# A hybrid decoder step on one core: roots ahead of conversions, the first gate slab in halves, a unit-wise tail, and sampled attention with stationary probabilities

## The chip, the cores and the metric

The kernel runs on one core of a Trainium2 chip. The metric is device time in microseconds, as the median of several executions. The profile is of one execution.

## The reference

One layer of a decoder for 256 prompt tokens and 8 sampled sequences of 4 tokens, 288 tokens in all. The input is normed and multiplied by `w_in` (2048 x 5632); eight heads go through a gated linear recurrence (HGRN2, state 128 x 128), sixteen query heads over four key heads through attention with a window of 128, a learned bias and a sink; both go through `w_out` and a SwiGLU.

```python
u = rms_norm(x, norm_g) @ w_in
qa, fa, ia, ga, qb, kb, vb = jnp.split(u, SPLIT_POINTS, axis=-1)
oa, st_p = hgrn2_scan(qa, lf, ka, va, state)       # prompt: zeros; sampled: state_hgrn
ob = swa(q, k, v, sink, bias, mask)                # sampled: over 128 cached keys + 4 new
x = x + jnp.concatenate([hgrn2_output(oa), ob], axis=-1) @ w_out
h = rms_norm(x, g)
y = x + (jax.nn.silu(h @ wg) * (h @ wu)) @ wd      # d_ff 5632
```

## The kernel before

All activations lie transposed: 128 features on the partitions, 288 tokens (`T`) on the free axis. Every weight is read once, in 192 slabs of 128 x 2048 numbers (1 MB). A slab takes three steps: SyncE loads it into one of three `raw` buffers; ScalarE rounds it to `wh` (`high`, L628), the high half; VectorE subtracts and gets the low half `wl` (`low`, L973). Activations have halves as well (`act_h`, `act_l`). TensorE's `passes` then does for each of 16 blocks of a slab high x high (L1514) and high x low (L1515), and after a wait for the low half (`between`) low x high (L1518): 48 matmuls of 288 columns into one PSUM bank. The load of slab s waits for the split of slab s - 3, the conversions wait through `unit_done` for TensorE's use of the buffer.

Slabs 0 to 43 are `w_in` (keys and queries of attention, f from 12, q from 20, i from 28, g from 36), 44 to 59 `w_out`, and then the FFN: gate and up slabs in turn, and down slabs of four output tiles each, chunk by chunk (`ffn_walk`). Each engine walks the same loop over s in an order written out by hand. TensorE does the small work at the start of a slab (`at_start`) and ahead of its low pass (`in_the_middle`).

Small work that the change touches, in order:

- Start: `x_squares` (ScalarE) sums squares of three token tiles, `root(1)` takes the root, VectorE inverts it, and `spread_rms` on TensorE in the middle of slab 2 spreads it over partitions. Only then can unit 0 be scaled on its way out of PSUM (`evacuate`), squared on ScalarE, and after it ScalarE did `high(3)`.
- Slab 10: `qk_rows` (mean of the q/k squares), `root(2)`, reciprocal; `qk_broadcast` (L1555) on TensorE in slabs 11 and 12, used by `qk_norm` on VectorE. `high(12)` stood at the end of step 9, `root(2)` in step 10.
- Slab 28 (`S_SA + 4`): sampled attention. `sampled_probs` transposes the probabilities, ScalarE copies them, `sampled_out` multiplies cached and new values (stationary, 64 columns) by them (16 columns moving), for each of four key heads one matmul of new tokens (L1656) and eight of cached ones (L1659). `s_out_copy` writes the head-major result `s_out`; `s_out_low` its low half. GpSimd then zeroes the level buffers, and after `s_out_low` loads the recurrence's states.
- Slabs 29 to 36 (`S_LV`): the recurrence's levels 0 to 7. `level` (L1690, sampled part L1701) computes products, `level_merge` (L1186) puts them under a mask, `level_up` (L1207, L1220 to L1222) scales q, k and f for the next. PSUM banks `mx` are shared, so TensorE waits for merges.
- `w_out`, then the first gate slab: `x2_high` and `x2_low` make the halves of the sixteen tiles of x. Tiles 8 to 15 go to the places that `w_out`'s last matmuls read, so they start after these. `passes_as_they_come` does all high blocks (L1528), `x2_ssq` (L1833), the low weights (L1531), the low activations (L1534).
- The end: `y_group` transposes four tiles of the result at a time (L1993), ScalarE and VectorE copy, SyncE stores; group 3 stands behind the last pass.

## Time and profile before

| | us |
|---|---|
| median of 3 runs (1365.98 to 1367.83) | 1367.4 |
| the profiled execution | 1367.65 |
| its span | 1365.9 |
| TensorE busy | 1352.0 |
| VectorE busy | 768.2 |
| ScalarE busy | 533.0 |
| GpSimd busy | 117.0 |

Times in rows are microseconds from the span's start. PE is TensorE's matmuls, PEld its weight loads, DVE VectorE, ACT ScalarE, POOL GpSimd, SP SyncE. A matmul in full single precision (`f32` operands that are not rounded) leaves two records. Records of matmuls overlap: the distance from start to start is the pace, the duration holds the latency too.

### The profile page before, as it was taken

How to read it: one execution, taken by the hardware profiler on the slowest of the kernel's cores; microseconds unless marked ns; L12 is line 12 of the kernel's file. 1: busy time of each engine (PE TensorE's matmuls, PEld its weight loads, DVE VectorE, ACT ScalarE, POOL GpSimd, SP SyncE). 2: the span in 40 equal slices, each digit the busy share in tenths (PEclk: the TensorE clock that was granted, in tenths of full speed). 3: DMA queues.
4: the chain of work that ended last, by engine and by line, in shares of the span. 5: the costliest groups of instructions: out<-in, count | busy, mean ns of one | idle time of the engine just before them, and what ended most of it. 6: DMA issues, size and time to landing. Idle time of an engine off the chain costs nothing.

```text
span 1365.9 us, 25119 instructions
## 1 busy us (share of the span) xinstructions
PE 1352.0 (99%) x11030; PEld 1317.2 (96%) x11030; DVE 768.2 (56%) x976; ACT 533.0 (39%) x615; POOL 117.0 (9%) x153
## 2 busy tenths in 40 slices
PE   9999999999999999999999999999999999999998
PEld 7999999898899999999999999999999999999998
DVE  5346765588737566446464555546464555545464
ACT  6337975323244344333333333333333333333331
POOL 2010430213200350000000000000000000000000
PEclk8999999899999999999999999999999999999999
DMA  9795545546853555555565565555565565555552
GB/s 286 198 311 156 162 130 151 154 112 180 245 201 124 185 155 155 163 177 155 161 179 155 173 166 156 164 175 155 163 177 155 168 171 156 164 174 155 164 176 71
DMA packets 320744, 231.42 MB, mean 169 GB/s; under 512 B 5126, under 2 KB 292111, under 8 KB 320314
## 3 DMA queue, kind: packets, MB, share of 16 engines
q1 hardware_dynamic: 314432, 206.19, 52.6%
q0 software_dynamic: 6112, 23.59, 5.3%
q8 instruction: 87, 1.43, 0.4%
q14 instruction: 23, 0.19, 0.0%
q10 hardware_dynamic: 90, 0.02, 0.0%
HBM read 219.99 MB, written 14.97 MB: 172 GB/s over the span
## 4 chain that ended last, share of the span: by engine, by line
PE 95%; DMA 2%; DVE 2%; issue 1%; ACT 1%; SPq 0%; ACTq 0%; DVEq 0%
PE acc L1514 29%; PE acc L1518 29%; PE acc L1515 28%; DMA raw<-in_w_in_dram 1%; PE mx L1464 1%; PE mx L1690 1%; PE acc L1528 1%; DMA reg_qkf<-in_x_sample_dram 1%; PE mx L1613 0%; PE mx L1585 0%; PE mx L1659 0%; DVE wl L973 0%; PE mx L1993 0%; PE mx L1773 0%; PE mx L1600 0%
## 5 line engine op out<-in xcount | busy, mean ns | idle before, releaser
L1514 PE MATMUL acc<-act_h,wh 128*128 128x288 f32 x2208 | 596.9, 299 | 1.1 <-ACT wh L628 1.1
L1515 PE MATMUL acc<-act_l,wh 128*128 128x288 f32 x2208 | 593.7, 295 | 0.0
L628 ACT ACTIVATE wh<-raw 128x2048 fp32r<-128x2048 f32 x192 | 366.8, 1911 | 248.3 <-PE acc L1518 234.5
L973 DVE TENSOR_TENSOR wl<-raw,wh 128x2048 fp32r<-128x2048 f32 x192 | 440.2, 2293 | 11.5 <-ACT wh L628 8.1
L1514 PEld LDWEIGHTS acc<-act_h,wh 128*128 128x128 f32 x2208 | 415.5, 188 | 7.2 <-issue 5.0
L1515 PEld LDWEIGHTS acc<-act_l,wh 128*128 128x128 f32 x2208 | 415.0, 188 | 0.0
L1518 PE MATMUL acc<-act_h,wl 128*128 128x288 f32 x2208 | 322.1, 298 | 0.0
L1518 PEld LDWEIGHTS acc<-act_h,wl 128*128 128x128 f32 x2208 | 302.1, 189 | 4.7 <-issue 3.3
L1514 PE MATMUL acc<-mix_h,wh 128*128 128x288 f32 x832 | 228.3, 299 | 0.0
L1515 PE MATMUL acc<-mix_l,wh 128*128 128x288 f32 x832 | 227.7, 295 | 0.0
L1514 PEld LDWEIGHTS acc<-mix_h,wh 128*128 128x128 f32 x832 | 157.1, 189 | 1.7 <-issue 1.7
L1515 PEld LDWEIGHTS acc<-mix_l,wh 128*128 128x128 f32 x832 | 156.4, 188 | 0.0
L1518 PE MATMUL acc<-mix_h,wl 128*128 128x288 f32 x832 | 142.1, 296 | 0.0
L1443 DVE TENSOR_TENSOR reg_x<-acc,reg_x 128x288 f32<-128x288 f32 x176 | 78.9, 455 | 96.9 <-PE acc L1518 96.9
L1518 PEld LDWEIGHTS acc<-mix_h,wl 128*128 128x128 f32 x832 | 120.3, 188 | 0.0
L929 ACT ACTIVATE reg_t<-reg_t 128x288 f32<-128x288 f32 x44 | 19.6, 446 | 186.2 <-DVE reg_t L1408 186.2
L1408 DVE TENSOR_TENSOR reg_t<-acc,reg_t 128x288 f32<-128x288 f32 x44 | 20.2, 459 | 127.3 <-PE acc L1518 127.2
L932 ACT ACTIVATE mix_h<-reg_t 128x288 fp32r<-128x288 f32 x44 | 19.6, 446 | 180.2 <-DVE reg_t L1416 180.2
L1416 DVE TENSOR_TENSOR reg_t<-acc,reg_t 128x288 f32<-128x288 f32 x44 | 20.2, 459 | 119.8 <-PE acc L1518 119.8
L1310 DVE TENSOR_TENSOR reg_x<-acc,reg_x 128x288 f32<-128x288 f32 x32 | 14.3, 453 | 37.5 <-PE acc L1518 37.5
L1420 DVE TENSOR_TENSOR mix_l<-reg_t,mix_h 128x288 fp32r<-128x288 f32 x44 | 20.2, 459 | 22.6 <-ACT mix_h L932 22.6
L1410 DVE TENSOR_TENSOR reg_t<-reg_t 128x288 f32<-128x288 f32 x44 | 20.2, 459 | 22.6 <-ACT reg_t L929 22.6
(265 smaller groups left out, 714.6 us busy)
## 6 DMA issues: line engine op xcount, KB each, us to landing
raw<-in_w_in_dram SPq DMA_DIRECT2D x44, 1024.0 KB, 5.9
raw<-in_w_gate_dram SPq DMA_DIRECT2D x44, 1024.0 KB, 5.6
raw<-in_w_up_dram SPq DMA_DIRECT2D x44, 1024.0 KB, 5.7
raw<-in_w_down_dram SPq DMA_DIRECT2D x44, 1024.0 KB, 5.1
raw<-in_w_out_dram SPq DMA_DIRECT2D x16, 1024.0 KB, 5.4
reg_x<-in_state_hgrn_dram POOLq DMA_DIRECT2D x16, 256.0 KB, 6.3
out_dram<-reg_x POOLq DMA_DIRECT2D x16, 256.0 KB, 3.5
bias_rows<-bias_line POOLq DMA_DIRECT2D x1, 3072.0 KB, 16.9
```

The costliest lines, as they stand in the source:

```text
L628: nc.scalar.activation(wh[:, s % WH, :], raw[:, s % RAW, :], ACT.Copy).then_inc(high_done, 1)
L929: nc.scalar.activation(tmp[:, 2 + t % 2, :], tmp[:, t % 2, :], ACT.Silu).then_inc(gate_silu, 1)
L932: nc.scalar.activation(mix_h[:, FC * (c % 2) + t, :], tmp[:, 4 + t % 2, :], ACT.Copy)\
L973: nc.vector.tensor_tensor(wl[:, s % WL, :], raw[:, s % RAW, :], wh[:, s % WH, :].bitcast(F32), ALU.subtract).then_inc(low_done, 1)
L1408: nc.vector.tensor_tensor(tmp[:, t % 2, :], ps, rstd2, ALU.mult).then_inc(gate_scaled, 1)
L1410: nc.vector.tensor_tensor(tmp[:, 2 + t % 2, :], tmp[:, 2 + t % 2, :], rstd2, ALU.mult)\
L1416: nc.vector.tensor_tensor(tmp[:, 4 + t % 2, :], ps, tmp[:, 2 + t % 2, :], ALU.mult)\
L1420: nc.vector.tensor_tensor(mix_l[:, slot, :], tmp[:, 4 + t % 2, :], mix_h[:, slot, :].bitcast(F32), ALU.subtract)\
L1443: nc.vector.tensor_tensor(xT[:, m, :], acc[n][:, 0:T], xT[:, m, :], ALU.add)\
L1514: mm(out, w_h[:, i, cols], a_hi[:, place(i), :], start=(i == 0), stop=False)
L1515: mm(out, w_h[:, i, cols], a_lo[:, place(i), :], start=False, stop=False)
L1518: ins = mm(out, w_l[:, i, cols], a_hi[:, place(i), :], start=False, stop=(i == k - 1))
```

## The change

1. `root(1)` stays behind the squares, but `x_squares` is split around `high(2)`, and `high(3)` follows the root directly. `root(2)` goes ahead of `high(12)`.
2. `sampled_out` holds the probabilities stationary (32 columns per key head, at four column positions) and moves 64 value columns, for each of eight sequences four matmuls of cached and four of new tokens. The result is token-major; ScalarE copies it (`s_tok_copy`), TensorE transposes it in eight pieces in slab 29 (`sampled_out_turned`), ScalarE and VectorE each take half of the evacuation. GpSimd's zeroing waits for `so_tok`, `s_out_low` moves to slab 30.
3. On VectorE, in slabs 29 to 32 `low` moves behind `level_merge` and `next_level`, and `lv_next` is given one product earlier.
4. The first gate slab runs in two halves of eight blocks (`passes_by_halves`), and `x2_ssq` behind it.
5. In the last down slab each output tile is transposed in the middle of the next tile's pass (`y_unit`), the copies and stores are of 384 and 128 columns; `y_group` 0 to 2 stand one unit earlier.

```diff
@@ -198,6 +198,7 @@
 s_new_t = reg_t[0:TS, 576:1600].rearrange("p (b m) -> p b m", b=NB)
+s_tok = reg_x[:, 0:512]
 s_out = reg_x[:, 640:896].rearrange("p (m t) -> p m t", m=8)
@@ -318,7 +319,10 @@
 so_done = sem("so_done")
+so_tok = sem("so_tok")
+so_t = sem("so_t")
 so_copied = sem("so_copied")
+so_copied_v = sem("so_copied_v")
 lb_sub = sem("lb_sub")
@@ -386,6 +390,14 @@
+def s_out_to(g, half):
+    to = s_out.rearrange("p (k m) (b l) -> p k m b l", k=KVH, b=NB)
+    return to[HD * (g % 2):HD * (g % 2) + HD, :, g // 2, 4 * half:4 * half + 4]
+
+def s_out_from(g, half):
+    src = acc[2 + half][0:HD, :].rearrange("p (b k m) -> p k b m", b=4, k=KVH)
+    return src[:, :, :, LB * g:LB * g + LB]
+
 block = ctx.enter_context(nc.Block())
@@ -456,14 +468,20 @@
     ffn_walk(gate_up, down)
-    for q in range(4):
-        cols = slice(512 * q, 512 * q + 512)
-        sp.wait_ge(yt_copied_a, 2 * q + 2)
-        sp.wait_ge(yt_copied_v, q + 1)
+    def store_y(cols):
         for j in range(2):
...
         sp.dma_start(y_sample.rearrange("b l d -> (b l) d")[:, cols], xtok[0:TS, 2, cols]).then_inc(y_out, 16)
-    sp.wait_ge(y_out, 16 * 12)
+
+    for q in range(3):
+        sp.wait_ge(yt_copied_a, 2 * q + 2)
+        sp.wait_ge(yt_copied_v, q + 1)
+        store_y(slice(512 * q, 512 * q + 512))
+    for n, cols in enumerate((slice(1536, 1920), slice(1920, 2048))):
+        sp.wait_ge(yt_copied_a, 8 + n)
+        sp.wait_ge(yt_copied_v, 4 + n)
+        store_y(cols)
+    sp.wait_ge(y_out, 16 * 15)
@@ -552,7 +570,7 @@
-    pool.wait_ge(so_copied, 2)
+    pool.wait_ge(so_tok, 1)
     nc.gpsimd.memset(reg_a[:, :], 0.0).then_inc(at_zero, 1)
@@ -628,9 +646,9 @@
-    def x_squares():
+    def x_squares(tiles):
         act.wait_ge(ssq_zero, 1)
-        for j in range(NTT):
+        for j in tiles:
             rows = P if j < 2 else TS
@@ -770,18 +788,18 @@
+    def s_tok_copy():
+        act.wait_ge(so_done, 1)
+        nc.scalar.activation(s_tok, mx[:, 0, :], ACT.Copy).then_inc(so_tok, 1)
+
     def s_out_copy():
-
-        act.wait_ge(so_done, 1)
-        src = mx[0:HD, 0, :].rearrange("p (k b m) -> p k b m", k=KVH, b=NB)
-        dst = s_out.rearrange("p (k m) (b l) -> p k m b l", k=KVH, b=NB)
+        act.wait_ge(so_t, 1)
         for g in range(G):
-            ins = nc.scalar.activation(dst[HD * (g % 2):HD * (g % 2) + HD, :, g // 2],
-                                       src[:, :, :, LB * g:LB * g + LB], ACT.Copy)
+            ins = nc.scalar.activation(s_out_to(g, 0), s_out_from(g, 0), ACT.Copy)
         ins.then_inc(so_copied, 1)
         act.wait_ge(so_copied, 1)
+        act.wait_ge(so_copied_v, 1)
         nc.scalar.activation(mix_h[:, :, TP:T], s_out, ACT.Copy).then_inc(so_copied, 1)
-
@@ -857,9 +875,11 @@
     high(1, None)
+    x_squares((0,))
     high(2, None)
-    x_squares()
+    x_squares((1, 2))
     root(1, rs)
+    high(3, units_through(0))
     for s in range(S_FFN):
@@ -875,6 +895,7 @@
             root(2, norm_rows)
+            high(s - 1 + WH, units_through(s - 1))
         if s == S_QKN:
@@ -886,6 +907,8 @@
             s_probs_copy(1)
+            s_tok_copy()
+        if s == S_SA + 5:
             s_out_copy()
@@ -913,7 +936,7 @@
                 x2_high(m)
-        if s < S_FFN - 1:
+        if s < S_FFN - 1 and s not in (0, S_QKN - 3):
             high(s + WH, units_through(s))
@@ -952,8 +975,14 @@
     ffn_walk(gate_up, down)
-    for q in range(4):
+    for q in range(3):
         y_copies(q)
+    act.wait_ge(yt_done, 4)
+    nc.scalar.activation(xtok[:, 0, 1536:1920], mx[:, 0, 0:384], ACT.Copy).then_inc(yt_copied_a, 1)
+    nc.scalar.activation(xtok[0:TS, 2, 1536:1920], mx[0:TS, 2, 0:384], ACT.Copy).then_inc(yt_copied_a, 1)
+    act.wait_ge(yt_done, 5)
+    nc.scalar.activation(xtok[:, 0:2, 1920:2048], mx[:, 3, 0:256].rearrange("p (j c) -> p j c", j=2), ACT.Copy)\
+        .then_inc(yt_copied_a, 1)
@@ -1164,6 +1193,12 @@
+    def s_out_copy():
+        dve.wait_ge(so_t, 2)
+        for g in range(G):
+            ins = nc.vector.tensor_copy(s_out_to(g, 1), s_out_from(g, 1))
+        ins.then_inc(so_copied_v, 1)
+
     def s_out_low():
@@ -1218,8 +1253,9 @@
         nc.vector.tensor_tensor(q_r, q_r, fb, ALU.mult)
-        link(nc.vector.tensor_tensor(k_l, k_l, fa, ALU.mult))
-        nc.vector.tensor_tensor(fl, fl, fr, ALU.mult).then_inc(lv_next, 1)
+        nc.vector.tensor_tensor(k_l, k_l, fa, ALU.mult).then_inc(lv_next, 1)
+        dve.wait_ge(lv_next, lv + 1)
+        link(nc.vector.tensor_tensor(fl, fl, fr, ALU.mult))
@@ -1355,7 +1391,9 @@
             s_softmax_back()
-        if s == S_SA + 4:
+        if s == S_SA + 5:
+            s_out_copy()
+        if s == S_SA + 6:
             s_out_low()
@@ -1364,7 +1402,7 @@
             next_level(s - S_LV)
-        if 0 <= s - S_SM - 1 < NU:
+        if S_LV <= s <= S_SM + NU:
             low(s - 1 + WL, units_through(s - 1))
@@ -1385,7 +1423,7 @@
         if not (S_SM <= s < S_SM + NU or s == S_FFN - 1):
-            if s:
+            if s and not S_LV - 1 <= s < S_SM:
                 low(s + WL, units_through(s))
@@ -1433,10 +1471,10 @@
         for i in range(DN):
-            if i and c == NCH - 1:
-                y_copy(i - 1)
             for n in range(4):
                 m = 4 * i + n
+                if n == 1 and i and c == NCH - 1:
+                    y_copy(i - 1)
                 if c:
@@ -1445,7 +1483,10 @@
     ffn_walk(gate_up, down)
-    y_copy(3)
+    dve.wait_ge(yt_done, 4)
+    nc.vector.tensor_copy(xtok[:, 1, 1536:1920], mx[:, 1, 0:384]).then_inc(yt_copied_v, 1)
+    dve.wait_ge(yt_done, 5)
+    nc.vector.tensor_copy(xtok[0:TS, 2, 1920:2048], acc[0][0:TS, 0:P]).then_inc(yt_copied_v, 1)
@@ -1532,6 +1573,25 @@
             ins = mm(out, w_h[:, i, :], act_l[:, place(i), :], start=False, stop=(i == KD - 1))
+        ins.then_inc(unit_done, 1)
+
+
+    def passes_by_halves(bank, s, high_sem, low_sem, place):
+
+        w_h = wh[:, s % WH, :].rearrange("p (k c) -> p k c", k=KD)
+        w_l = wl[:, s % WL, :].rearrange("p (k c) -> p k c", k=KD)
+        out = acc[bank][:, 0:T]
+        for half in (range(8), range(8, KD)):
+            for i in half:
+                pe.wait_ge(high_sem, i + 1)
+                mm(out, w_h[:, i, :], act_h[:, place(i), :], start=(i == 0), stop=False)
+            if half[0] == 0:
+                pe.wait_ge(low_done, s + 1)
+            for i in half:
+                mm(out, w_l[:, i, :], act_h[:, place(i), :], start=False, stop=False)
+            for i in half:
+                pe.wait_ge(low_sem, i + 1)
+                ins = mm(out, w_h[:, i, :], act_l[:, place(i), :], start=False, stop=(i == KD - 1))
         ins.then_inc(unit_done, 1)
@@ -1651,15 +1711,24 @@
         pe.wait_ge(vc_in, 16)
-        out = mx[0:HD, 0, :].rearrange("p (k b m) -> p k b m", k=KVH, b=NB)
-        for k in range(KVH):
-            mm(out[:, k], v_tok[0:TS, 2, HD * k:HD * k + HD], s_new_t[:, :, 32 * k:32 * k + 16],
-               start=True, stop=True)
-            for b in range(NB):
-                ins = mm(out[:, k, b], v_cache[:, b, HD * k:HD * k + HD], s_probs_t[:, b, 32 * k:32 * k + 16],
-                         start=False, stop=True, skip_group_check=True)
+        out = mx[:, 0, :].rearrange("p (b d) -> p b d", b=NB)
+        for b in range(NB):
+            for k in range(KVH):
+                mm(out[32 * k:32 * k + 32, b], s_probs_t[:, b, 32 * k:32 * k + 32],
+                   v_cache[:, b, HD * k:HD * k + HD], start=True, stop=False)
+            for k in range(KVH):
+                ins = mm(out[32 * k:32 * k + 32, b], s_new_t[:, b, 32 * k:32 * k + 32],
+                         v_tok[0:TS, 2, HD * k:HD * k + HD], start=False, stop=True)
         ins.then_inc(so_done, 1)
...
+    def sampled_out_turned():
+        pe.wait_ge(so_tok, 1)
+        pe.wait_ge(z_made, AH + 28 - S_Q)
+        for b in range(NB):
+            ins = nc.tensor.transpose(acc[2 + b // 4][0:HD, P * (b % 4):P * (b % 4) + P],
+                                      s_tok[:, HD * b:HD * b + HD], ident)
+            if b % 4 == 3:
+                ins.then_inc(so_t, 1)
@@ -1669,7 +1738,7 @@
             pe.wait_ge(k_made, AH)
-            pe.wait_ge(so_copied, 2)
+            pe.wait_ge(so_tok, 1)
         if lv == 1:
@@ -1728,6 +1797,8 @@
         states_taken(S_SM + 4 * g, 2)
+        pe.wait_ge(so_copied, 1)
+        pe.wait_ge(so_copied_v, 1)
         pe.wait_ge(is_made, HG * g + HG)
@@ -1848,6 +1919,8 @@
             sampled_probs()
+        if s == S_SA + 5:
+            sampled_out_turned()
         if 0 <= s - S_LV < 8:
@@ -1972,12 +2045,11 @@
             def between():
-                if first:
-                    x2_ssq()
                 pe.wait_ge(low_done, s + 1)
...
             if first:
-                passes_as_they_come(bank, gu_slab(c), xgh_done, xgl_done, between, x2_place)
+                passes_by_halves(bank, gu_slab(c), xgh_done, xgl_done, x2_place)
+                x2_ssq()
             else:
@@ -1994,6 +2066,24 @@
+    def y_unit(i):
+
+        pe.wait_ge(down_added, 16 * (NCH - 1) + 12 + i + 1)
+        if i == 0:
+            pe.wait_ge(yt_copied_a, 6)
+            pe.wait_ge(yt_copied_v, 3)
+        for j in range(NTT):
+            rows = P if j < 2 else TS
+            if i < 3:
+                out = mx[0:rows, j, P * i:P * i + P]
+            elif j < 2:
+                out = mx[:, 3, P * j:P * j + P]
+            else:
+                out = acc[0][0:TS, 0:P]
+            ins = nc.tensor.transpose(out, xT[:, 12 + i, P * j:P * j + rows], ident)
+        if i >= 2:
+            ins.then_inc(yt_done, 1)
+
     def down(c):
@@ -2010,14 +2100,21 @@
                     pe.wait_ge(inner_done if n % 2 else gate_scaled, (c + 1) * FC + 2 + n // 2 + 1)
+                last = c == NCH - 1 and i == DN - 1
+
+                def between():
+                    if n == 0:
+                        pe.wait_ge(low_done, s + 1)
+                    if last and n:
+                        y_unit(n - 1)
+
                 passes(n, dn_slab(c) + i, FC, slice(P * n, P * n + P), mix_h[:, half:half + FC, :],
-                       mix_l[:, half:half + FC, :],
-                       lambda: pe.wait_ge(low_done, s + 1) if n == 0 else None)
-                if n == 1 and i and c == NCH - 1:
+                       mix_l[:, half:half + FC, :], between)
+                if n == 0 and i and c == NCH - 1:
                     y_group(i - 1)
...
     ffn_walk(gate_up, down)
-    y_group(3)
+    y_unit(3)
```

## Rows read from the trace of the kernel before

**Rows 1.** The page: busy time, share of the span and instructions, by engine.

```profile
PE 1352.0 (99%) x11030; PEld 1317.2 (96%) x11030; DVE 768.2 (56%) x976; ACT 533.0 (39%) x615; POOL 117.0 (9%) x153
```

**Rows 2.** Windows, FFN: span; busy (records) of PE, PEld, DVE, ACT, POOL; clock; DMA share; GB/s.

```profile
520.00:1340.00 820.00, 820.00 (x6154) 819.99 (x6153) 434.35 (x468) 276.84 (x216) 0.00 (x0) 1.00 0.57 164
```

**Rows 3.** Timeline, ACT and PE (start, duration, what, idle before and releaser); window.

```profile
42.43 0.45 ACT L667 ACTIVATE reg_t<-reg_g 128x288 f32<-128x288 f32 x1 [9.05 <-DVE reg_g L1052]
...
44.73 0.40 PE L1514 MATMUL acc<-act_h,wh 128*128 128x288 f32 x1 [1.12 <-ACT wh L628]
...
40.00:45.00 5.00, 3.88 (x31) 3.65 (x30) 1.58 (x4) 2.57 (x4) 0.00 (x0) 1.00 0.00 1
```

**Rows 4.** Timeline of ACT and PE, slabs 8 to 12.

```profile
97.44 1.91 ACT L628 ACTIVATE wh<-raw 128x2048 fp32r<-128x2048 f32 x1 [4.86 <-DMA raw<-in_w_in_dram]
...
99.73 0.68 PE L1543 MATMUL mx<-reg_t,small 128*32 128x288 f32 x4 [1.14 <-ACT reg_t L667]
...
104.22 0.44 ACT L653 ACTIVATE reg_t<-reg_t 128x288 f32<-128x288 f32 x1
...
106.92 0.77 PE L1555 MATMUL mx<-reg_t,reg_a 32*128 32x288 f32 x8
...
109.94 1.72 PE L1555 MATMUL mx<-reg_t,reg_a 32*128 32x288 f32 x8
```

**Rows 5.** Timeline of PE, slabs 28 and 29.

```profile
248.47 0.43 PE L1656 MATMUL mx<-reg_t,reg_v 32*64 32x128 f32 x2
...
254.30 1.89 PE L1659 MATMUL mx<-reg_x 128*64 128x16 f32 x16
...
256.12 4.21 PE L1518 MATMUL acc<-act_h,wl 128*128 128x288 f32 x16
...
260.26 1.75 PE L1690 MATMUL mx<-reg_qkf 128*32 128x32 f32 x128
...
263.44 0.64 PE L1701 MATMUL mx<-reg_qkf 128*32 128x128 f32 x16 [1.43 <-DVE reg_a L1186]
```

**Rows 6.** Windows around sampled attention's output (clock stands before the DMA share).

```profile
242.30:251.25 8.95, 8.95 (x86) 8.29 (x84) 4.21 (x5) 5.14 (x7) 0.00 (x0) 1.00 0.87 227
...
251.25:261.40 10.15, 10.15 (x138) 9.14 (x140) 1.46 (x3) 2.25 (x7) 3.55 (x3) 0.50 0.03 8
...
262.00:264.00 2.00, 0.57 (x17) 0.38 (x16) 2.00 (x4) 0.83 (x1) 2.00 (x4) 1.00 0.84 223
```

**Rows 7.** Timeline of PE, level 1; one line's weight loads (ns, min/median/max).

```profile
273.11 0.41 PE L1701 MATMUL mx<-reg_qkf 128*32 128x64 f32 x15
...
L1701 PEld LDWEIGHTS mx<-reg_qkf x48: 106/109/113, 263.4 to 281.5; 128*32 128x32 f32 x48
```

**Rows 8.** Timeline of DVE and PE, slabs 29 to 32.

```profile
260.47 2.28 DVE L973 TENSOR_TENSOR wl<-raw,wh 128x2048 fp32r<-128x2048 f32 x1
...
272.96 0.28 PE L1690 MATMUL mx<-reg_qkf 128*32 128x16 f32 x11 [1.18 <-issue]
...
289.19 1.29 PE L1690 MATMUL mx<-reg_qkf 128*32 128x16 f32 x128 [0.59 <-DVE reg_qkf L1222]
```

**Rows 9.** Timeline of PE, ACT and DVE, first gate slab.

```profile
507.88 4.23 PE L1528 MATMUL acc<-act_h,wh 128*128 128x288 f32 x16
...
508.14 3.52 ACT L841 ACTIVATE act_h<-reg_x,gains 128x288 fp32r<-128x288 f32 x8 [3.63 <-PE acc L1518]
...
508.52 5.32 DVE L1315 SCALAR_TENSOR_TENSOR act_l<-reg_x,gains,act_h 128x288 fp32r<-128x288 f32 x10
...
516.68 0.29 PE L1514 MATMUL acc<-act_h,wh 128*128 128x288 f32 x1
```

**Rows 10.** Timeline of PE, ACT and SP, the end.

```profile
1359.72 1.53 PE L1993 MATMUL mx<-small,reg_x 128*128 128x128 f32 x12 [0.62 <-DVE reg_x L1443]
...
1361.28 1.06 ACT L951 ACTIVATE reg_qkf<-mx 128x512 f32<-128x512 f32 x2 [4.28 <-PE mx L1993]
...
1362.37 0.81 SPq L464 DMA_DIRECT2D out_dram<-reg_qkf  x2
```

## The prediction

> **What bounds the kernel now.** I began with the page. TensorE is busy for 99% of the span and VectorE for 56% [rows 1], so the others matter only where TensorE waits for them. What is to be seen next is that the matmuls of the slabs have nothing to give: in the FFN the windows show TensorE busy for all of 820 us, with 6154 records in them, 0.133 us each [rows 2]; a slab has 48, so 6.40 us. 192 slabs of 6.40 us are 1228.8 us of 1365.9. The other 137 us are the start, the small matmuls between slabs, waits, a stretch at half clock and the end. The change leaves the slabs' matmuls alone, so I read the timeline of TensorE outside the FFN for idle time and slow stretches, and then those of ScalarE and VectorE at each one for what was late.
>
> **Slab 3 (high(3) ahead of the loop).** TensorE stands idle for 1.12 us for ScalarE's conversion of slab 3 [rows 3]. ScalarE does it right behind the square of the first unit at 42.43, which needs the spread root; ahead of that square it had sat idle for 9.05 us, since the root itself. The new place is right behind that root. The unit it waits for is done by then, and the raw slab by my reading is in, as transfers are at a standstill from 40 us [rows 3]. So the conversion ends near 35.3. VectorE's split of slab 3, which now starts at the conversion's end at 44.7, then starts behind the first two evacuations at about 42.75 and is ready at 45, before the middle of slab 3 (43.6 + 4.4 = 48.0). Gain **1.1 us**. Squares of tile 0 ahead of high(2) are costed at nothing: high(2) then ends near 27.5, and slab 2 starts at 36.39; without that cover it would be at most one conversion, 1.9 us. The conversion and the three squares end at the same time, and the root with them.
>
> **Slab 12 (root(2) ahead of high(12)).** ScalarE waits for slab 12's transfer, converts it, then loads a table and takes the root at 104.22; VectorE's reciprocal follows, and the q/k norms come late. The second group of eight broadcasts takes 109.94 to 111.59, 1.65 us, where the first eight take 0.70 [rows 4]. With the root first, the table load starts at 99.7 and the root waits only for VectorE's mean square. That stands behind the split of slab 11, which starts when high(11) ends (97.44 + 1.91) and takes 2.3, so the mean square ends near 102.1. All of the chain moves 2.1 us forward, more than the 0.95 us that is waited. high(12) ends at 104.5 and is wanted at 109. Gain **1.0 us**. The idle 1.14 us at 99.73 stays: it hangs on the square of unit 9, behind high(11), which waited 4.86 us for its transfer [rows 4]. Slabs are requested by VectorE's splits, which follow TensorE, so I let that wait move with the rest. If transfers do not move, it grows and swallows both gains (second rival).
>
> **Sampled attention's output.** Old: four groups of 2 L1656 and 16 L1659 matmuls, 72 records from 248.47 to 256.19, **7.7 us**. The clock stood at 1.0 up to 251.25 and at 0.5 (1.2 GHz of 2.4) from there, though TensorE had not been idle; what it did before the fall was 2.8 us of these thin matmuls [rows 5, 6]. New: 64 matmuls, two records each as everywhere in this precision, 128 in all, with 32 stationary columns at four column positions in turn and 64 moving columns. For the half over 128 rows the trace has just this form: L1701 with 64 columns: 15 records that take 0.41 us with the latency of the last, and the slab behind them begins 0.34 us after the first, so at most 24 ns each [rows 7]. The half over 32 rows has no row. Bounds: 10 ns as L1690 (128 records in 1.29 us [rows 8]), and 0.21 us as L1656 (two in 0.43 us [rows 5]), which is one column position and twice the columns. I take 24 ns for both, since the four column positions make it like L1701: 128 x 0.024 = **3.1 us**. Ends: 1.3 us, and 1.5 + 64 x 0.21 = 15 us. Gain 4.6 us.
>
> If the clock holds, the 16 L1518 behind it take 2.13 us in place of 4.14 (256.12 to 260.26), gain **2.0**, and the 128 L1690 of level 0 take 1.3 in place of 1.75, gain **0.4**. For: the stretch from 262.0 to 264.0 has TensorE busy for 0.57 us of 2.00 and was granted 1.0 [rows 6], and the new matmuls fill four column positions at a time. Added: eight transposes at about 0.11 us (twelve in 1.53 us with their latency [rows 10]), cost **-0.9**. Their evacuation, four small instructions each on ScalarE and VectorE, lies beside level 0.
>
> Then level 0's last block waits for VectorE's first merge, 1.43 us idle. VectorE was in the 2.28 us split begun at 260.47 [rows 5, 8]. That split now follows the merge and level_up. The new chain runs: output done 251.6, copy 0.6, GpSimd's memsets 3.0 (they now hang on so_tok) until 255.3, one merge 0.65, so 256.0. TensorE gets there at 251.6 + 2.1 + 0.9 + 1.3 = 255.9. The idle time falls to about 0.3, gain **1.1**. In all 4.6 + 2.0 + 0.4 - 0.9 + 1.1 = **7.2 us**.
>
> **Levels 1 to 3.** Level 3 waits 0.59 us at 289.19 for VectorE's last product of level_up [rows 8]. Merge and level_up now come ahead of the split, 2.2 us earlier, and lv_next comes one instruction earlier (1.2 us): gain **0.6**. The splits of slabs 30 to 33 end later in return: by my chain, with the 2.1 us of the slabs before left out, at 263.0, 273.2, 282.1 and 288.8, and TensorE wants them at about 269, 278, 286.5 and 295.5, so at least 4 us are left. Behind the moved split on VectorE stand evacuations of the next unit; the tightest, unit 30, is 1.3 us late but its bank is wanted a slab later. The low half of the sampled output moves to slab 30, and with it the eight state loads on GpSimd's queue, to about 264 to 270; the first is read near 286. The gap of 1.18 us inside level 1 has no releaser ("issue") and falls in that burst of loads [rows 8]. I leave it in, as the burst now starts just at level 1; 0 to 1.2 us for the range.
>
> **First gate slab.** TensorE takes it from 507.88 to 516.68, 8.80 us. Its first 16 matmuls take 4.1 us (4.23 with their latency), since eight high halves come off ScalarE every 0.43 us from 508.14 (3.52 us), and the low halves off VectorE until 513.8 [rows 9]. By halves, tiles 0 to 7 give 24 matmuls that are ready, 3.2 us until 511.1. The high of tile k of the rest is there at 508.6 + 0.44k, the last at 511.7, wanted at 512.0; the last low at 513.85, wanted at 514.15. So no wait: 6.40 us and 0.3 for the two ssq matmuls. Gain 8.80 - 6.70 = **2.1 us**. The ssq result comes at 514.7 in place of 512.2; VectorE gets to it only near 516.0, behind the 2.3 us split of slab 61 that follows the low halves [rows 9], so nothing is later. Slab 62 wants its split at 525.3; it is done at 522.5. If the low halves slip by more than 0.3 us, that goes off the gain; floor 1.5.
>
> **The end.** Nine of the last twelve transposes move in front of the last pass, 0.9 us later for that pass. Then 0.62 us wait, three transposes (about 0.5 in place of 1.53), one copy of 256 columns (0.4 in place of 1.06 for two), and issue and landing as before (3.5 us from 1362.37 to the end of the span) [rows 10]. Saved 1.0 + 0.7 - 0.9 = 0.8. A new wait: y_unit(0) needs ScalarE's two copies of group 2, ready 1.06 + 0.3 us after the transposes, while only eight matmuls (1.07 us) lie between: 0.3. Gain **0.5**; ends 0 and 1.
>
> **Sum.** 1.1 + 1.0 + 7.2 + 0.6 + 2.1 + 0.5 = 12.5 us. The profiled execution took 1367.65 (span 1365.9), the median is 1367.4: the sum gives 1355.15 against the one, and **1354.9** against the other, which I forecast.
>
> **Rivals.**
> *The clock falls all the same* (0.22). The new block is still 3 us without a slab matmul, and what follows includes transposes. For: the only fall in mid-kernel stands at this place. Against: the levels' matmuls, as small, ran at 1.0 (at 262 to 264 with 1.43 us of idle time beside them). Price 2.0 + 0.4 back, and about 0.6 for a part of the block and its transposes: 1357.9. The Trainium skill (TensorE: Matmul & The Clock Gate, Part 4) says that a transpose "doesn't count as PE-busy the same way", which speaks for this rival; here the stretch from 242.3, which begins with sixteen records of transposes and goes on with a slab's matmuls, kept 1.0 up to 251.25 [rows 6].
> *Transfers stay where they are* (0.12). The wait at slab 10 grows by what slab 3 gained, and the next one by the rest: 2.1 us back, 1357.0. For: the wait for slab 11's transfer was 4.86 us [rows 4]. Against: they stand still at 40, and every request there follows TensorE.
> *The tiled matmuls are bound by their weight loads* (0.07). L1701's loads are 109 ns each [rows 7]; one after another, 128 are 14.0 us in place of 3.1: 1365.8, no measurable change. Against: its 15 records took 0.34 us and not 1.6, so loads overlapped. The Trainium skill (the same page, Part 3) says that loads overlap matmuls "only when row_grp differs", and here only the column group differs; the row decides against it.
> *Slower* (0.03): the half clock, once fallen, holds on through slabs. Each costs 6.4 us more, so from 15.2 us, 2.4 slabs, it is slower by over 0.2%; four slabs give 1380.5. The one fall here ended after ten us, with a slab's matmuls running.
> My forecast has 0.56; its own range, with 1 us on either side of the sampled block and of the waits, is 1352.5 to 1357. Within 0.2% (2.7 us) is about what cannot be told from no change. Faster 0.56 + 0.22 + 0.12 = 0.90 and 0.01 of the third rival, 0.91; same its other 0.06; slower 0.03. Range 1351.4 (the output's matmuls at 10 ns, 1.8; issue gap gone, 1.2; end 0.5) to 1360.5 (first two rivals together, and 0.5 of the gate slab).
>
> **What would show it.** No idle before slab 3; the second L1555 group at 0.7 us; the new output matmuls in 3 us, clock 1.0 there, L1518 behind them 2.1 us; slab 29 starting some 9.4 us earlier (264.0 to 254.7); gate slab and ssq 6.7 us; last output transfer issued 3.5 us before the end. It is wrong if the 32-row matmuls take over 50 ns, if the clock falls, or if the wait at slab 10 is over 2 us.

## The result, and the profile after

The changed kernel takes 1361.26 us (median of 20 runs, 1354.61 to 1364.64) against 1365.66 us before (20 runs on the same chip, 1359.95 to 1368.45): ratio 0.9967, 95% interval 0.9955 to 0.998. It is faster, by 4.4 us where 12.5 were forecast, and its time lies outside the forecast's range. (The forecast started from 1367.4 us, the median of three runs; 1.7 of the 6.4 us between the forecast 1354.9 and the measured time are that.) The profiled execution has a span of 1357.0 us and a mean granted clock of 0.997.

The spans of the two profiles differ by 8.9 us, the medians by 4.4, so the start comes first. Before's profile had a granted clock of 0.5 there (windows of 2 us, from about 13 to 26 us), after's had 1.0. The main pass of slab 3, the first 32 of its 48 matmuls, starts at 38.99 and not at 44.73 [rows 3]; of these 5.74 us, 1.12 are the idle time that is gone, and some 4.6 I put down to the clock. It does not look like the change's doing: in both kernels the executions with a mean clock of 0.999 have the short spans (1352.8 and 1353.2 after, 1357.7 to 1358.8 before) and those with 0.991 to 0.992 the long ones (1360.0 to 1362.8, and 1363.9 to 1367.9 in the runs of before beside the first experiments). From here on I compare stretches inside the kernel.

The timeline of TensorE in the changed kernel, at slabs 3, 10 and 12 (start, duration, what, idle before it and its releaser), against [rows 3, 4]:

```profile
38.99 0.29 PE L1555 MATMUL acc<-act_h,wh 128*128 128x288 f32 x1
...
93.67 0.44 PE L1603 MATMUL mx<-reg_t,small 128*32 128x288 f32 x2 [0.81 <-ACT reg_t L685]
...
103.88 0.77 PE L1615 MATMUL mx<-reg_t,reg_a 32*128 32x288 f32 x8
104.57 0.40 PE L1555 MATMUL acc<-act_h,wh 128*128 128x288 f32 x1
```

No idle ahead of slab 3. The second group of eight broadcasts takes 0.69 us to the next instruction, 1.65 before; the wait at slab 10 has gone down by 0.33, not up. The transfers did move.

The same view at sampled attention's output, against [rows 5], and its windows, against [rows 6] (the clock stands ahead of the DMA share):

```profile
244.77 0.32 PE L1717 MATMUL mx<-reg_x 128*32 128x64 f32 x8
245.02 0.31 PE L1720 MATMUL mx<-reg_v,reg_t 32*32 32x64 f32 x8
245.26 3.92 PE L1559 MATMUL acc<-act_h,wl 128*128 128x288 f32 x16
249.02 1.04 PE L1728 MATMUL acc<-small,reg_x 128*64 128x128 f32 x8
249.99 1.35 PE L1759 MATMUL mx<-reg_qkf 128*32 128x32 f32 x128
251.82 0.65 PE L1770 MATMUL mx<-reg_qkf 128*32 128x128 f32 x16 [0.48 <-DVE reg_a L1221]
252.39 0.40 PE L1555 MATMUL acc<-act_h,wh 128*128 128x288 f32 x1
```

```profile
238.90:245.30 6.40, 6.40 (x148) 4.76 (x146) 0.46 (x2) 2.09 (x5) 0.00 (x0) 1.00 1.04 263
245.40:248.70 3.30, 3.30 (x14) 3.30 (x15) 0.00 (x0) 0.60 (x1) 2.65 (x2) 0.50 0.02 5
248.80:253.00 4.20, 3.72 (x159) 3.19 (x159) 3.03 (x9) 3.36 (x7) 0.16 (x1) 1.00 0.02 4
```

Sixteen groups of eight records, L1717 and L1720 in turn, begin 0.245 us after each other, from 241.32 to 245.26: 3.9 us for 7.7. Then the clock is at half for 3.4 us all the same, and the 16 low matmuls take 3.76 us for 4.14. From slab 28's main pass to slab 29's it is 15.5 us (20.0 before).

What follows has become slower. From slab 29's main pass to slab 33's it is 41.03 us, where it was 36.51 (264.02 to 300.53). TensorE's timeline of levels 1 and 2, against [rows 7, 8]:

```profile
265.61 0.33 PE L1794 MATMUL mx<-small,reg_t 128*128 128x128 f32 x1 [0.50 <-issue]
267.99 1.15 PE L1759 MATMUL mx<-reg_qkf 128*32 128x16 f32 x110
273.00 0.46 PE L1759 MATMUL mx<-reg_qkf 128*32 128x16 f32 x18 [3.86 <-issue]
```

3.86 us of idle time inside level 2, behind 110 of its 128 records, with no releaser ("issue": the engine waited for nothing that the profile names), and from 272.7 on some 3.4 us at half clock. The wait of 0.59 us in level 3 is gone. Next to it the timeline of GpSimd, which issues the state loads, and 2 us windows of all engines:

```profile
259.91 5.95 POOL L583 DMA_DIRECT2D reg_x<-in_state_hgrn_dram  x8 [10.95 <-DVE mix_l L1204]
```

```profile
266.00:268.00 2.00, 2.00 (x18) 1.83 (x16) 1.97 (x2) 0.63 (x2) 0.00 (x0) 1.00 1.03 289
268.00:270.00 2.00, 1.13 (x111) 1.03 (x111) 2.00 (x3) 0.99 (x2) 0.00 (x0) 1.00 1.03 289
270.00:272.00 2.00, 0.00 (x0) 0.00 (x0) 0.14 (x1) 1.19 (x1) 0.00 (x0) 1.00 1.08 281
```

In the last window TensorE stands still and VectorE nearly so (0.14 of 2 us), while the DMA engines are full.

The first gate slab in the timeline, against [rows 9]: 501.01 to 507.68, 6.67 us for 8.80, in six groups of eight without a wait.

```profile
501.01 1.23 PE L1587 MATMUL acc<-act_h,wh 128*128 128x288 f32 x8
...
507.41 0.65 PE L1904 MATMUL mx<-reg_t,reg_a 128*128 128x288 f32 x2
507.68 0.51 PE L1555 MATMUL acc<-act_h,wh 128*128 128x288 f32 x1
```

And the end, timelines of TensorE, VectorE and SyncE, against [rows 10]:

```profile
1350.60 0.49 PE L2083 MATMUL mx<-small,reg_x 128*128 128x128 f32 x3
...
1351.72 0.46 DVE L1481 TENSOR_TENSOR reg_x<-acc,reg_x 128x288 f32<-128x288 f32 x1 [1.44 <-PE acc L1559]
1352.09 0.55 DVE L1487 COPY reg_qkf<-mx 128x384 f32<-128x384 f32 x1
1352.23 0.44 PE L2083 MATMUL mx<-small,reg_x 128*128 128x128 f32 x2 [0.62 <-DVE reg_x L1481]
...
1352.71 0.81 SPq L473 DMA_DIRECT2D out_dram<-reg_qkf  x2
1353.57 0.44 SPq L474 DMA_DIRECT2D out_dram<-reg_qkf  x1
1354.11 0.84 SPq L473 DMA_DIRECT2D out_dram<-reg_qkf  x2
1354.99 0.43 SPq L474 DMA_DIRECT2D out_dram<-reg_qkf  x1
```

From the last transposes to the end of the span: 4.77 us, 6.18 before. Ahead of that point three groups of transposes were put in, 0.31 us each (they start 1.91 us apart, of which twelve matmuls are 1.60), with 0.13 us of waiting, so 6.18 - 4.77 - 0.93 - 0.13, some 0.3 us, are gained. SyncE's six issues take 2.7 us in a row, and the first waits for VectorE's copy of 384 columns, which stands behind the last addition.

By these stretches the change gives 1.12 + 0.33 + 0.97 + 4.5 - 4.5 + 2.1 + 0.3 = 4.8 us. The medians say 4.4.

### The profile page after: what moved, and what is told of

Read it like the earlier page. It is cut to its first block, busy times and chain, and to the rows that moved or that the text cites. A ratio compares the mean times of both kernels' runs of the same rounds, so it can differ in the third digit from the quotient of the medians.

```text
span 1357.0 us, 25263 instructions
## 1 busy us (share of the span) xinstructions
PE 1342.7 (99%) x11094; PEld 1310.5 (97%) x11094; DVE 770.4 (57%) x981; ACT 533.1 (39%) x617; POOL 119.4 (9%) x153
## 3 DMA queue, kind: packets, MB, share of 16 engines
q8 instruction: 88, 1.44, 0.4%
## 4 chain that ended last, share of the span: by engine, by line
PE 95%; DMA 2%; DVE 1%; ACT 1%; issue 1%; SPq 0%; DVEq 0%
PE acc L1555 30%; PE acc L1559 29%; PE acc L1556 29%; DMA raw<-in_w_in_dram 2%; PE mx L1759 1%; PE mx L1673 0%; PE mx L1645 0%; PE mx L1844 0%; PE mx L1660 0%; DVE wl L1002 0%; PE mx L1817 0%; PE mx L2065 0%; PE mx L1879 0%; PE mx L1690 0%; PE mx L1697 0%
## 5 line engine op out<-in xcount | busy, mean ns | idle before, releaser
L1081 DVE TENSOR_TENSOR reg_g<-acc,rstd 128x288 f32<-128x288 f32 x16 | 7.2, 457 | 45.6 <-PE acc L1559 45.6
```

## The experiments

Each experiment is named by x and its number, and the code cuts show only the lines that matter ("..." stands for lines left out). They are cut from the changed kernel, but for x2 and x7, which start from the kernel before. The question is where 4.5 us in the levels went. First theory: TensorE waits for its own instructions. The page has the instructions of each engine, and in its list of DMA queues (packets, MB, share) one of kind "instruction":

```profile
PE 1342.7 (99%) x11094; PEld 1310.5 (97%) x11094; DVE 770.4 (57%) x981; ACT 533.1 (39%) x617; POOL 119.4 (9%) x153
...
q8 instruction: 88, 1.44, 0.4%
```

88 packets in 1.44 MB are 16 KB each; 11094 pairs of matmul and weight load over 88 are 126, so by my reading a packet is 128 pairs, and a few records have none or are missing; between the gaps that end at 265.61 and at 273.00 the timeline has 1 + 16 + 110 = 127. One such packet moves in the trace from 270.51 to 271.74, and TensorE goes on at 273.00. Level 2 takes 128 pairs in 1.3 us, matmuls of slabs take them in 17 us.

The DMA records of all fourteen profiles, before's and those of the experiments below included, bear this out. In the FFN, where TensorE takes 128 pairs in 128 x 0.133 = 17.0 us, the 16 KB packets of this queue are 16.8 to 17.0 us apart in the mean. Between 200 and 320 us these profiles have 28 gaps of TensorE of over 0.1 us marked issue, and each of the 28 ends 1.2 to 1.6 us behind the landing of such a packet. A packet itself takes 0.9 to 1.5 us there, DMA engines full or not; what grows is the time before it starts to move.

**State loads made tiny (x1).** Slots 0 to 3 load one row of 128 (the rest of the buffer is zeroed instead; the sampled results and states that come of it are not the reference's). TensorE's instructions are as in the changed kernel.

```
+ rows = slice(0, 1 if u < 4 else P)
- pool.dma_start(s0[:, u % 4, :, bb], states_of(state_hgrn, u, bb))
+ pool.dma_start(s0[rows, u % 4, :, bb], states_of(state_hgrn, u, bb)[rows])
...
+ nc.gpsimd.memset(reg_x[:, 0:4096], 0.0)
```

> The changed kernel, but the first eight state loads move one row in place of 128 (GpSimd zeroes the buffer first), so the sampled recurrence starts from other numbers. Theory A (TensorE's instructions come over the same transfer engines and wait behind the burst of state loads): both gaps of TensorE marked issue in slabs 30 and 31 (0.50 and 3.86 us) shrink to under 0.3 us each, and the half clock after the second one is gone; slab 33 begins about 5 us earlier relative to slab 29. Theory B (the levels' short matmuls run through their instructions faster than they can be fetched, whatever else is moved): a gap of at least 1 us stays in level 1 or 2.

Measured in one execution: 1352.08 us, span 1350.3, clock 0.999 (the fast start; after's spans with that clock are 1352.8 and 1353.2). TensorE's timeline in level 2:

```profile
266.33 1.15 PE L1762 MATMUL mx<-reg_qkf 128*32 128x16 f32 x110
268.04 0.33 PE L1762 MATMUL mx<-reg_qkf 128*32 128x16 f32 x18 [0.56 <-issue]
```

The gap stands behind the same 110th record, and is 0.56 us and not 3.86, where theory A had under 0.3; 0.54 us stand in slab 30 (0.50 in the changed kernel), and a gap of 1.06 us in level 0, which the changed kernel does not have, comes while the DMA engines are idle. Slab 29 to slab 33 takes 36.01 us for 41.03. So the place comes from the instruction stream, and most of the length of the long gap from the transfers; some wait is left without them.

**Before, with the loads later (x2).** The kernel before, with s_out_low at slab 30 and not at 28, so that the loads start at 272.99 and not at 260.70.

```
- if s == S_SA + 4:
+ if s == S_SA + 6:
      s_out_low()
```

> The kernel before with one thing changed: the low half of the sampled output, on which the state loads hang, is made in slab 30 in place of slab 28, so the burst of eight loads starts some 8 us later. Theory A: the gap of 1.18 us in level 1 goes and one of 2 to 4 us comes in level 2, with or without a fall of the clock; the kernel is 1 to 4 us slower than before. Theory B: the gap stays as it is, time unchanged.

1368.94 us (12 runs), before 1366.89 (23 runs), ratio 1.0003 (0.9984 to 1.0023). The 1.18 us of level 1 are gone; 1.81 us of issue stand in slab 31's matmuls, 0.47 in level 3, and 1.05 us of waiting for level_up in level 2. Slab 29 to 33: 38.25 us, 1.7 more than before. The gap wanders with the loads, though not into level 2 as theory A had it, but the price alone is too small to show in the ratio.

**Early state loads (x3).** Six of the eight loads right behind the zeroing; only slot 0 needs what the low half of the output frees.

```
+ for u in range(1, 4):
+     load_state(u)
  pool.wait_ge(mixl_done, 2 * KVH + 1)
  pool.wait_ge(outs, 16 * TOKEN_OUTS)
- for u in range(4):
-     load_state(u)
+ load_state(0)
```

> The changed kernel with six of the eight state loads issued right behind GpSimd's zeroing, where transfers stand still, and only the two of slot 0 (which holds the sampled output) behind its low half. Theory A: at slab 31 there is at most 1 us of issue gap, slab 33 begins 3.5 to 5 us earlier relative to slab 29, and the whole is 3.5 to 5 us faster than the changed kernel, so about 8 to 9 us (0.6%) faster than before. Theory B: no change against the changed kernel (ratio 0.9967).

1356.95 us (6 runs), ratio 0.9929 (0.9903 to 0.9954). Level 2 is one group of 128 records without a gap; 1.07 us of issue in level 0 and 0.70 ahead of it at slab 30 are left. Slab 29 to 33: 35.65 us.

**Sampled output in two pieces (x4).** For the clock: four sequences on either side of eight low matmuls.

```
- for b in range(NB):
+ for b in range(4 * half, 4 * half + 4):
...
+ if halfway and i == k // 2:
+     halfway()
...
```

> The changed kernel with sampled attention's output matmuls in two pieces, four sequences ahead of slab 28's low pass and four in the middle of it, 1.07 us of slab matmuls between. Theory C (the clock fell because thin matmuls stood together for 4 us): granted clock 1.0 through slab 28, the 16 low matmuls take 2.13 us besides the piece between them, 1.6 us gained, of which up to 1 us is given back as GpSimd's zeroing and the merge come 1.1 us later. Rival: the clock falls on any stretch with this much thin work, and nothing is gained.

1362.78 us (12 runs), ratio 0.9975 (0.9954 to 0.9996). The clock stayed at 1.0, but so it did in the two kernels above with the block whole, so the cut is not shown to be the reason. The gap in level 2 is here too, 4.10 us, with 6.8 us of half clock at and behind it: slab 29 to 33 takes 42.3 us.

**More work at the start (x5).** Two matmuls behind each of the sixteen groups of x transposes.

```
  ins.then_inc(xt_done, 1)
+ for _ in range(2):
+     mm(acc[0][:, 0:P], ones, ones, start=True, stop=True)
```

> The changed kernel with two 128x128 matmuls (nobody reads them; their bank is written afresh later) behind each group of x transposes at the start, to keep TensorE busy there. Theory A, the difference between the spans of the two profiles beside the medians is the start's clock: before's profile had a granted clock of 0.5 from 12.3 to 26.0 us, after's 1.0, and slab 3's main pass began at 44.73 and 38.99, of which only 1.12 us is the change. If the half clock at the start follows from thin work of TensorE, the added columns keep the clock at 1.0 and slab 3 begins near 39; the median of many runs falls by 1 to 4 us (ratio 0.990 to 0.995) and lies close to the fastest. Theory B, the clock at the start is chance and does not follow the work: ratio as the changed kernel, 0.9967 (0.9955 to 0.998), with the same spread of 10 us, and the profile shows 0.5 at the start as often.

1360.41 us (12 runs), ratio 0.9976 (0.9954 to 0.9998). The profiled execution has 1.0 at the start, and slab 1 starts some 7 us later for the added matmuls, which eat what the clock gives; 7 of 12 executions had a mean clock of 0.997 or more (7 of 20 of the changed kernel), yet others fell to 0.989. So it is not shown that the added work made the full clock more frequent; it did not make it sure, and did not pay. What I had not asked for is worth more: its timeline has no issue gap from slab 28 to slab 32. Slab 28 to 29 takes 13.98 us and slab 29 to 33 takes 34.92, though the state loads come as in the changed kernel. The 64 records added moved every later instruction half a packet; that this hit a good place was luck, and x9 tests it.

**VectorE's copy ahead of the last addition (x6).**

```
+ if c == NCH - 1 and m == KD - 1:
+     dve.wait_ge(yt_done, 4)
+     nc.vector.tensor_copy(xtok[:, 1, 1536:1920], mx[:, 1, 0:384]).then_inc(yt_copied_v, 1)
...
```

> The changed kernel with VectorE's copy of 384 columns of the output ahead of its last addition, no longer behind it. Theory A, the tail gained 0.15 us and not 0.5 because that copy (started 352 ns late, behind the last addition) holds back SyncE's first three stores, and SyncE's issues of some 0.43 us each are the end's bound: the first group is issued 0.3 to 0.6 us earlier, and the stretch from the last output matmul's group to the end is 0.3 to 0.6 us shorter than the 4.77 us of the changed kernel. Theory B, the last addition is now later by the copy and the three last transposes with it, so that the last group's stores gain nothing: the stretch is 4.77 us or up to 0.3 longer. Either is below what a ratio of medians shows (0.04%), so the profile decides.

1359.79 us (6 runs), ratio 0.9947 (0.9926 to 0.9968). SyncE's timeline, the first three of its last four rows:

```profile
1348.29 0.81 SPq L473 DMA_DIRECT2D out_dram<-reg_qkf  x2
1349.14 0.44 SPq L474 DMA_DIRECT2D out_dram<-reg_qkf  x1
1349.68 0.84 SPq L473 DMA_DIRECT2D out_dram<-reg_qkf  x2
```

The last transposes start at 1348.52, the span ends at 1352.5: 3.98 us for 4.77. The spans are rounded to 0.1 here, so 0.7 to 0.8 us are gained, more than the 0.3 to 0.6 expected. The last addition stands 1.12 us behind the transposes ahead of it, as in the changed kernel; the copy fits in front of it. This profile also shows the levels with 1.30, 0.42 and 3.03 us of issue.

**Three parts alone (x7).** The kernel before, with the roots ahead of the conversions and the gate slab by halves.

```
- if s < S_FFN - 1:
+ if s < S_FFN - 1 and s not in (0, S_QKN - 3):
...
- passes_as_they_come(bank, gu_slab(c), xgh_done, xgl_done, between, x2_place)
+ passes_by_halves(bank, gu_slab(c), xgh_done, xgl_done, x2_place)
+ x2_ssq()
...
```

> Kernel before with three parts of the change alone: roots ahead of conversions at both places, and the first gate slab in halves with the sums of squares behind it. The sampled output, the levels and the tail are as before. By the traces these parts are worth 1.12 + 0.33 + 0.97 + 2.13 = 4.5 us: theory A (the sampled part gives 4.5 us and the levels give them back) expects 1361.2 us against 1365.7, ratio 0.9967, the same as the whole change. Theory B (the sampled part's gain survives, and the other parts are worth less than their stretches show, since a later wait takes them back) expects a ratio of 0.998 to 1.000.

1358.85 us (10 runs), before 1365.71 (25 runs), ratio 0.9955 (0.9933 to 0.9978), with theory A's 0.9967 inside and theory B's 0.998 to 1.000 outside. It is as fast as the whole change: sampled output, levels and tail together give nothing that these runs can tell from zero.

**Early loads, tail copy and the added matmuls together (x8).**

```
  x3 + x6 + x5, edits as above
```

> The changed kernel with the three edits together: six of the eight first state loads right behind the zeroing, VectorE's copy ahead of the last addition, and the added matmuls at the start. The early loads alone measured 1356.95 us, ratio 0.9929. Theory A, each edit's gain is on the path: 4.4 us for the loads, 0.3 for the tail, 1 to 4 for the start: 1351 to 1355 us, ratio 0.988 to 0.992. Theory B, only the loads count: ratio 0.993.

1360.55 us (10 runs), ratio 0.997 (0.9953 to 0.9987): neither theory. Early loads lose their point where the stream already stands well (slab 29 to 33: 34.52, against 34.92 without them), and the 7 us at the start stay.

**The stream moved by half a packet (x9).** In the stretch in which TensorE waits for x anyway, 52 matmuls of 32x32 in place of 20 of 128x128; each is two records, so 64 pairs more. They take 5.3 us, the 20 took 7.4, so TensorE has no more to do.

```
- mm(mx[:, 0, 0:P], ones, ones, start=True, stop=True)
+ mm(mx[0:32, 0, 0:32], ones[:, 0:32], ones[:, 0:32], start=True, stop=True)
- warm(10)
+ warm(26)
```

> The changed kernel with the 20 warm-up matmuls of 128x128 ahead of the x tiles made into 52 of 32x32: 32 matmuls and their weight loads more in TensorE's instruction stream, in time in which TensorE waits for x anyway, so that every later instruction stands half a 16 KB packet further on in the stream, at no cost in time; that is also how far the kernel with the added matmuls at the start had moved it, which had no issue gap in the levels although its state loads came as late as the changed kernel's. Theory A, the gap is where the end of a fetched piece of the stream falls in a fast stretch (level: 128 matmuls and 128 loads in 1.5 us) while the state loads fill the queues: the gaps in levels 0 to 3 vanish or move, slab 29's to slab 33's main pass takes 34.9 to 36 us instead of 41.0 (or 38.4 in another run), and the median falls by 3 to 6 us: ratio 0.992 to 0.995. Theory B, the phase does not matter: 3 to 4 us of issue in level 2 again, ratio 0.9967.

1356.82 us (5 runs), before 1366.35 (18 runs), ratio 0.9942 (0.9916 to 0.9969). TensorE's timeline from level 2 into slab 31:

```profile
270.51 1.26 PE L1759 MATMUL mx<-reg_qkf 128*32 128x16 f32 x126
271.64 0.42 PE L1770 MATMUL mx<-reg_qkf 128*32 128x64 f32 x14
...
276.45 0.40 PE L1555 MATMUL acc<-act_h,wh 128*128 128x288 f32 x1 [0.19 <-issue]
```

All of level 2 without a gap; what is left up to slab 33 are 0.19 us in slab 31 and 0.20 in level 3. Slab 29 to 33: 35.34 us. Its executions with a mean clock of 0.993 have spans of 1354.6 and 1355.0; those of the changed kernel with that clock have 1359.0 to 1359.8, 4.5 us more, with the same loads at the same place against slab 30. The smaller matmuls may have a price elsewhere: none of the 11 executions of this kernel and of x11 has a mean clock above 0.995, where 7 of 20 of the changed kernel have 0.997 or more. No run here separates that from chance.

**Moved by three quarters of a packet (x10).** The same with `warm(34)`: 96 pairs more than the changed kernel.

> The same with 68 small matmuls in the warm-up (48 more than the changed kernel, some three quarters of a packet of instructions). Theory A: the gaps stand elsewhere again than in the changed kernel and than with 52; where they come to lie isn't forecast, the sum of issue gaps between 240 and 300 us differs from 4.4 us by over 1 us. Theory B: 3 to 4 us in level 2 as before. If 68 small ones outlast the wait for x, slab 1 begins up to 2 us later.

1362.77 us (10 runs, one of which took 2607.33), ratio 0.9975 (0.9958 to 0.9992).

```profile
273.51 0.40 PE L1770 MATMUL mx<-reg_qkf 128*32 128x64 f32 x12
277.96 0.37 PE L1770 MATMUL mx<-reg_qkf 128*32 128x64 f32 x2 [4.06 <-issue]
```

The gap is back, 4.06 us, so theory A's number (a sum of gaps over 1 us away from 4.4) did not come. Its place did move, and can be counted. In the changed kernel it stands behind record 110 of level 2. With packets of 128 pairs and 96 pairs more ahead, the next border is at 110 - 96 + 128 = 142. Here 128 records of L1759 and 14 of L1770 (12 in the row shown, two interleaved ahead of it) are done when it stops: 142. With 64 more it is 110 - 64 + 128 = 174, past the 144 records of level 2 and 30 records into slab 31, 4.0 us at 0.133: the 0.19 us at 276.45 above.

**Early loads, tail copy, stream moved by half a packet (x11).**

```
  x3 + x6 + x9, edits as above
```

> The changed kernel with the early state loads, VectorE's copy ahead of the last addition, and 52 small warm-up matmuls. Theory A, the gains stack: early loads alone measured 0.9929 against before, the tail's copy perhaps 0.3 us more, the moved stream up to 1.8 us more (the two gaps left there): 1353 to 1356 us, ratio 0.990 to 0.993. Theory B, the loads already took all that the moved stream can give: 0.993, as the same kernel without the small matmuls.

1356.5 us (6 runs), ratio 0.9932 (0.9912 to 0.9952). By the median theory B, no more than the early loads alone; the interval holds a part of A as well. Slab 29 to 33 takes 34.5 us, 1.15 less than with the early loads alone.

**Early loads and tail copy (x12).**

```
  x3 + x6, edits as above
```

> The changed kernel with the early state loads and VectorE's copy ahead of the last addition, warm-up as it was. Expected as the early loads alone, 0.9929 (0.9903 to 0.9954), and up to 0.3 us faster by the end. The profile shows whether the level 2 gap of 3 to 4 us stays away in a second kernel with early loads. Rival: early loads only moved the burst and the stream's packets by chance, and the gap is back: 0.996.

1352.59 us (6 runs), ratio 0.9914 (0.9891 to 0.9937), the lowest ratio of all. It has the changed kernel's stream. Level 2 in TensorE's timeline, and the windows:

```profile
267.85 1.15 PE L1761 MATMUL mx<-reg_qkf 128*32 128x16 f32 x110
269.29 0.33 PE L1761 MATMUL mx<-reg_qkf 128*32 128x16 f32 x18 [0.30 <-issue]
```

```profile
266.00:268.00 2.00, 2.00 (x32) 1.83 (x34) 1.97 (x2) 0.52 (x2) 0.00 (x0) 1.00 0.04 10
268.00:270.00 2.00, 1.70 (x145) 1.50 (x139) 1.88 (x4) 1.33 (x2) 0.00 (x0) 1.00 0.09 24
```

Record 110 again, 0.30 us, and a DMA share of 0.04 to 0.09 where it was 1.03. Slab 29 to 33: 35.95 us. Between this kernel and the moved stream with the same edits the intervals overlap, and four of the six executions here had the full clock at the start. The other two, with a mean clock of 0.995, have spans of 1354.4 and 1355.4; five of the six of x11 have 0.993 or 0.994 and 1354.0 to 1355.1. Which of the two is better is open.

All profiles in one table (us from main pass to main pass; "clock" is the lowest granted between slabs 28 and 29; x2 and x7 have the old block):

```
                     slab 28 to 29   clock   slab 29 to 33   gap in level 2
before                  19.99         0.5       36.51            -
x2 before, late         20.01         0.5       38.25            -
x7 three parts          18.53         0.5       36.42            -
after                   15.51         0.5       41.03            3.86
x12 early, tail         15.52         0.5       35.95            0.30
x10 stream 3/4          15.47         0.5       40.41            4.06
x8                      15.46         0.5       34.52            -
x1 tiny                 14.86         1.0       36.01            0.56
x6 tail                 14.82         1.0       38.37            3.03
x4 output split         14.77         1.0       42.28            4.10
x3 early                14.72         1.0       35.65            -
x5, x9, x11             13.98         1.0       34.92, 35.34, 34.50   -
```

## Why the prediction was wrong

**The wrong step** is in the part on the levels: the issue gap of 1.18 us was kept at its size ("I leave it in, as the burst now starts just at level 1"), with 0 to 1.2 us for the range. It is a wait for TensorE's next 16 KB of instructions, and it grows with what TensorE gains. In after's profile the border of one packet is crossed at 265.61 (the 0.50 us there is its own wait; 128 pairs ahead of the next), and the next packet is wanted at 269.14, 3.5 us later. It starts to move only at 270.51, 4.9 us after 265.61, has landed at 271.74, and lets TensorE go on at 273.00, 7.4 us after 265.61. In x12 the packet starts 1.2 us behind that border. Without the burst the way from border to border takes 3.8 us (x12: 265.47 to 269.29) and 4.1 (x1: 263.94 to 268.04).

The burst is in the way because the loads did not follow. TensorE reaches level 2 12.3 us earlier than before (267.99 for 280.27; 7.15 us of it come from ahead of slab 28), but the loads start only 0.8 us earlier (259.91 for 260.70), since their release had been put two slabs later, from slab 28 to slab 30. Before, the DMA engines were idle again when level 2 began (a share of 0.04 to 0.05 from 278 to 282 us); now level 2 lies inside the burst. Of the 4.5 us lost (41.03 - 36.51), 3.86 + 0.50 + 0.20 are gaps and 1.7 the half clock behind them, less the 1.18 and 0.59 that went. Shown by four kernels: smaller or earlier loads with the same stream (x1, x12) shrink the gap to 0.56 and 0.30 us, a moved stream with the same loads (x9) leaves none in level 2, another move (x10) brings it back where the count of 128 says. That the packet starts late because it queues behind the loads' packets in the same DMA engines fits the windows, but is not shown; the records don't name the engine.

**Sampled output, forecast 7.2, got 4.5 in this profile.** Matmuls: 3.94 us, 31 ns each where I took 24 for both halves; 0.8 us too little. The rows of 32 and of 128 cost the same. The clock: the first rival (it falls all the same) came true in 4 of 11 profiles with the new block, and in 3 of 3 with the old one, where it lasted 7 to 10 us and now 3.4. Price in the low matmuls 1.6 us (3.76 for 2.13). Where neither the clock nor a packet is in the way (x5, x9, x11), the block is 6.0 us shorter: 7.2 less the 0.8 of the matmuls, 0.2 of the merge wait (0.48, forecast 0.3) and 0.2 that I can't place. Where the clock fell, 1.5 more are gone. Where it held and the stream stood as in the changed kernel (x1, x3, x4, x6), an issue gap of 0.9 to 1.3 us behind record 114 of level 0 took 0.7 to 0.9: TensorE had run into the next border early. So the mechanism of the matmuls was right and their size 0.8 off, and with the changed kernel's stream the block has won 5.3 us at best (x3). The Trainium skill (TensorE: Matmul & The Clock Gate, Part 4) says that a transpose "doesn't count as PE-busy the same way"; the fall here comes at 245.35, after 3.9 us of thin matmuls and ahead of the transposes, so it neither supports nor refutes that.

**The load-bound rival** is refuted: 128 records in 3.94 us, where loads of 109 ns in a row would be 14. The Trainium skill (the same page, Part 3) has loads overlap "only when row_grp differs"; in L1717 all loads fill the same rows and differ in their columns alone, and they overlap at 31 ns though one takes 106 to 109. The measurement decides.

**Slab 3** 1.1: 1.12. **Slab 12** 1.0: 0.97, and 0.33 more at slab 10; the rival of the transfers fell. **Gate slab** 2.1: 2.13, 6.67 us where I had 6.70. x7 has these 4.5 us alone; its ratio allows 3.0 to 9.2. **Levels** 0.6: the wait of 0.59 went as forecast; without gaps (x5, x9) the stretch is 1.2 to 1.6 us shorter, 0.59 and most of the 1.18. **The end** 0.5: 0.3. I had priced the wait, the transposes and the copy, and not that SyncE's first issue hangs on a copy queued behind the last addition; one moved copy gives 0.7 to 0.8 us.

**The sum.** 12.5 less 4.5 + 0.6 in the levels, 2.7 in the block and 0.2 at the end, plus 0.33: 4.8. With the loads out of the way and the copy moved (x12) the ratio is 0.9914 (0.9891 to 0.9937), and the forecast was 1354.9 / 1367.4 = 0.9909: what I forecast was within reach of another kernel than mine.

## What to carry to other kernels

A gap named "issue" inside a run of short matmuls may be the instruction stream: count the records between two such gaps, and look for a DMA burst under them. Whatever makes TensorE earlier must move the bulk loads as well, out of the stretches with short instructions; here a release put two slabs later, with everything ahead of it faster, cost as much as a whole rewritten block had won. Before two profiles are subtracted, compare the clock at their starts, and subtract stretches, not spans.

## What the runs showed of the hardware

- TensorE's instructions come in 16 KB packets, 128 matmul and load pairs. From crossing one border to going on behind the next takes 3.8 to 4.1 us with little other traffic (x12, x1), and with the DMA engines full 5.5 (x9, 270.97 to 276.45; x10, 272.5 to 277.96), 7.4 (after) and 7.7 us (x4, 270.62 to 278.28). TensorE goes on 1.2 to 1.6 us behind a packet's landing (28 gaps of 28). Slab matmuls use up a packet in 17 us, a level in 1.3.
- The place of a gap can be counted to the record (110, 142, 174), and 64 more cheap pairs in an idle stretch at the start took 5.7 us out of slabs 29 to 33 (41.03 to 35.34); the ratios are 0.9967 and 0.9942, with intervals that overlap.
- The clock fell with TensorE uninterrupted, behind 3.5 to 4.3 us of 64-column matmuls in a 32-column tile, in 4 of the 11 kernels profiled with this block, one execution each. A gap of 3.0 to 4.1 us was followed by 3.4 to 6.8 us of half clock in three of four cases (after, x4, x10; not x6).
- Matmuls with 32 stationary columns at four column positions and 64 moving ones run at 31 ns a record, with 128 rows as with 32.
